# A hybrid decoder trunk on one core: the low halves of the last projection tile's weights move from VectorE to GpSimd

## The reference

```python
h = rms_norm(x, ln1_g[layer])
(a_q, a_ckv, a_kr, i_q, i_k, i_w, b_u, c_q, c_kv, c_gate) = jnp.split(h @ w_in[layer], offsets, axis=-1)
a_out = dsa_mixer(...)    # sparse attention with an indexer's top 64, rotary on parts
b_out = s5_mixer(b_u, ...)  # diagonal state-space model: scan over the positions
c_out = nsa_mixer(...)    # compressed, selected and window attention
x = x + concat(rms_norm(a_out), rms_norm(b_out), rms_norm(c_out)) @ w_out[layer]
x = x + square(relu(rms_norm(x, ln2_g[layer]) @ w_up[layer])) @ w_down[layer]
```

## Time and profile before

| | us |
|---|---|
| median of 3 runs (800.11 to 800.49) | 800.15 |
| the profiled execution | 800.82 |
| its span | 798.8 |
| busy: TensorE / VectorE / ScalarE / GpSimd | 687.8 / 524.1 / 362.2 / 316.4 |

### The profile page before, as it was taken

How to read it: one execution, slowest core, us unless ns; L and a number is a source line. 1 busy time by engine, 2 the same in 40 slices (tenths; PEclk the granted TensorE clock), 3 DMA queues, 4 the chain that set the end, 5 groups by cost and what they waited for, 6 DMA issues and landing times.

```text
span 798.8 us, 11006 instructions
## 1 busy us (share of the span) xinstructions
PE 687.8 (86%) x4020; PEld 606.3 (76%) x4020; DVE 524.1 (66%) x925; ACT 362.2 (45%) x656; POOL 316.4 (40%) x485
## 2 busy tenths in 40 slices
PE   2881944988989999999999697597998999999994
PEld 2771833976879999999978585476788999999983
DVE  5629999486385555666557999768447645555553
ACT  3550142366554454444436316155735544444441
POOL 5699993255305349999000444335510000000000
PEclk9995885799999999999999988689999999999998
DMA  9530310010168556556635350000125566666631
GB/s 258 172 105 0 111 52 1 1 53 27 54 185 246 196 186 185 167 184 201 210 108 169 105 163 1 1 27 27 54 89 166 167 203 191 187 185 188 186 127 80
DMA packets 51876, 100.25 MB, mean 126 GB/s; under 512 B 11093, under 2 KB 15902, under 8 KB 51822
## 3 DMA queue, kind: packets, MB, share of 16 engines
q1 hardware_dynamic: 48750, 96.40, 39.0%
q0 software_dynamic: 720, 1.97, 1.0%
q10 hardware_dynamic: 2352, 1.18, 0.6%
HBM read 98.48 MB, written 1.05 MB: 125 GB/s over the span
## 4 chain that ended last, share of the span: by engine, by line
PE 61%; DVE 25%; issue 6%; POOL 4%; ACT 2%; DMA 1%; DVEq 0%; SPq 0%; ACTq 0%; POOLq 0%
PE pb L1408 61%; DVE dtmp L978 6%; DVE w_lo L1051 4%; DVE scan L1119 2%; DVE dtmp L985 1%; DVE x L985 1%; DVE btab L1320 1%; POOL e L519 1%; DVE h_lo L985 1%; POOL bt L519 1%; DMA pos_i<-in_positions 1%; DVE top L1204 1%; DVE scan L978 1%; ACT btab L884 1%; DVE dtmp L1109 1%
## 5 line engine op out<-in xcount | busy, mean ns | idle before, releaser
L1051 DVE TENSOR_TENSOR w_lo<-raw,w_hi 128x1024 fp32r<-128x1024 f32 (+2 forms) x176 | 220.1, 1268 | 140.5 <-ACT w_hi L725 140.2
L725 ACT ACTIVATE w_hi<-raw 128x1024 fp32r<-128x1024 f32 (+2 forms) x184 | 188.2, 1028 | 255.0 <-PE pb L1408 255.0
L1408 PE MATMUL pb<-h_hi,w_hi 128*128 128x256 f32 x512 | 145.0, 283 | 1.8 <-DVE h_lo L985 1.8
L1408 PE MATMUL pb<-h_lo,w_hi 128*128 128x256 f32 x512 | 144.9, 283 | 0.0
L1408 PE MATMUL pb<-h_hi,w_lo 128*128 128x256 f32 x512 | 144.9, 283 | 0.0
L523 POOL TENSOR_SCALAR pst<-stat 128x2 f32<-128x2 f32 (+1 forms) x11 | 2.8, 255 | 307.5 <-ACT proj L729 278.7
L1408 PE MATMUL pb<-w_hi,h_hi 128*128 128x512 f32 (+2 forms) x224 | 86.0, 384 | 21.3 <-DVE w_lo L1051 20.4
L1408 PEld LDWEIGHTS pb<-h_hi,w_hi 128*128 128x128 f32 x512 | 98.2, 192 | 2.7 <-DVE w_lo L1051 2.2
L1408 PE MATMUL pb<-w_hi,z_hi 128*128 128x512 f32 x256 | 99.8, 390 | 0.0
L1408 PE MATMUL pb<-w_hi,z_lo 128*128 128x512 f32 x256 | 99.8, 390 | 0.0
L1408 PE MATMUL pb<-w_lo,z_hi 128*128 128x512 f32 x256 | 99.6, 389 | 0.0
(11 more groups left out here) (267 smaller groups left out, 1212.2 us busy)
## 6 DMA issues: line engine op xcount, KB each, us to landing
raw<-in_w_up SPq DMA_DIRECT2D x64, 512.0 KB, 3.8
raw<-in_w_down SPq DMA_DIRECT2D x64, 512.0 KB, 4.3
raw<-in_w_in SPq DMA_DIRECT2D x24, 512.0 KB, 4.6
raw<-in_w_out SPq DMA_DIRECT2D x16, 512.0 KB, 3.8
raw<-in_w_in SPq DMA_DIRECT2D x8, 308.0 KB, 3.1
raw<-in_w_in SPq DMA_DIRECT2D x8, 280.0 KB, 3.2
x<-in_x ACTq DMA_DIRECT2D x1, 1024.0 KB, 5.3
out<-x SPq DMA_DIRECT2D x2, 512.0 KB, 2.7
```

The source lines that it names most:

```text
L725: hi_made.by(act.activation(w_hi[:, n % RING, 0:width(n)], raw[:, n % RING, 0:width(n)], ACT.Copy))
L1051: lo_made.by(dve.tensor_tensor(w_lo[:, n % RING, 0:width(n)], raw[:, n % RING, 0:width(n)], w_hi[:, n % RING, 0:width(n)].bitcast(F32), AL ...
L1408: return pe.matmul(o, l, r, start=start, stop=stop, skip_group_check=True)
```

## The change

`lo_out` is defined ahead of the rotations, takes the width of the piece, and GpSimd calls it for pieces 16 to 19 between its rotations 1 and 2. VectorE's four calls between its rounds 1 and 2 go. This holds for both layers.

```diff
@@ GpSimd
                 rstd(L, 2, rkv[:], stat[:, 2:4], A_RANK)
+                def lo_out(n):
+
+                    pool.wait_ge(lo_made.sem, lo_made.at(L, n))
+                    pool.wait_ge(hi_made.sem, hi_made.at(L, n + 1))
+                    lo_made.by(pool.tensor_tensor(w_lo[:, n % RING, 0:width(n)], raw[:, n % RING, 0:width(n)],
+                                                  w_hi[:, n % RING, 0:width(n)].bitcast(F32), ALU.subtract))
+
+
                 for r in range(ROUNDS):
+                    if r == 2:
+                        for n in range(16, 20):
+                            lo_out(n)
                     pool.wait_ge(scanned.sem, scanned.at(L, r + 1))
...
-                def lo_out(n):
-
-                    pool.wait_ge(lo_made.sem, lo_made.at(L, n))
-                    pool.wait_ge(hi_made.sem, hi_made.at(L, n + 1))
-                    lo_made.by(pool.tensor_tensor(w_lo[:, n % RING, :], raw[:, n % RING, :],
-                                                  w_hi[:, n % RING, :].bitcast(F32), ALU.subtract))
...
@@ VectorE
                 for n in range(12, 16):
                     lo(n)
                 s5_round(1)
-                for n in range(16, 20):
-                    lo(n)
                 s5_round(2)
```

## The result

The changed kernel takes 810.34 us (median of four runs, 808.65 to 811.0) against 800.32 us: the ratio is 1.012, with a 95% interval from 1.0102 to 1.0138. It is slower by 10.0 us. The kernel before was run a fourth time beside it, so its median here is 800.32 and not 800.15. The profiled execution took 810.84 us.

What follows compares the result with a forecast made beforehand. The prediction took VectorE's queue to bound the kernel before the rotary block, with tile 4 becoming late; 5.4 us in layer 0 plus 3.0 in layer 1 made 8.4, so a median of 808.5 us, range 805.0 to 813.5.

Steps and rivals of the forecast that it cites:

- What bounds, and the slack: VectorE's queue sets the pace before the rotary block; tile 4's result has slack of 10.5 us in layer 0, 2.3 in layer 1.
- the two terms expected: Expected for "late" before its run: round 3 plus 2.6 us in layer 0, plus 1.3 to 1.7 in layer 1.
- GpSimd's price: One 560-column subtraction on GpSimd takes 1.45 us with VectorE idle, 1.7 beside its scans; bounds 1.3 and 2.0.
- Layer 0: Tile 4 waits for subtractions behind rotation 1; the rotary block ends near 126.2 instead of 120.76: +5.4 us, bounds +4 and +8.5.
- Layer 1: Subtractions run beside round 2's scans, tile 4 is late; the block ends at 494.9 instead of 491.89: +3.0 us, +2 to +4.9.
- The recovery in the block: In layer 0 rotation 2 slows only the rotary block's first 2.7 us; the rest runs undisturbed, against 7.9 us in all before.
- The first rival: GpSimd slows VectorE through the late block, 7.9 us wherever it starts: +8.5 and +4.9, 813.5 us; chance 0.13.
- hidden wait: Rival: block without GpSimd beside it and tile 4 at full clock, +0.7 and -2.1, about 799 us, no change; chance 0.04.
- relief: Rival: VectorE loses 3.7 us in layer 0, 0.4 in layer 1 if tile 4 is out in time: 796.1 us; chance 0.03.
- What was to cost nothing: Loads of pieces 20 to 23, `bu(3)`, the indexer's work, ScalarE's copies and the wider `lo_out` add no time.
- the margin of 3 us: In layer 0 the indexer's results come at about 129.7, before VectorE reads them after round 3 at some 132.5.
- a stretch between the layers that grows by more than 1 us: Sign of a wrong forecast: stretches behind 138.85 and its layer 1 counterpart grow or shrink by more than a microsecond.

Runs made afterwards that it cites:

- Layer 0 only: The change made in layer 0 alone, layer 1 as in the kernel before: 805.97 us, ratio 1.0079.
- layer 1 only: The change made in layer 1 alone, layer 0 as in the kernel before: 804.39 us, ratio 1.0053.
- late: The kernel before with one more wait: TensorE begins tile 4 only when GpSimd has ended rotation 1; 804.98 us, ratio 1.005.
- 8 columns: The changed kernel with each of GpSimd's four subtractions covering only 8 of 560 columns, the rest left out: 802.44 us, ratio 1.003.

## Why the prediction was right

It had 808.5 us, from 805.0 to 813.5, and slower at 0.93; measured were 810.34 and a second time 810.3. The chain from GpSimd's place in its queue over tile 4 and the block to round 3 is what the trace shows. The sum of the two layers, 8.4 us, was met at 8.3 in part because two errors cancel: layer 0 came out 0.5 lower and layer 1 0.4 higher.

*What bounds, and the slack.* VectorE's queue sets the pace, tile 4 has a slack of 10.5 and 2.3 us, and GpSimd's place behind rotation 1 overdraws it. "Layer 0 only", "layer 1 only" and "late" confirm it with costs in both layers, the 3.8 us of "late" against 3.9 to 4.3 by the two terms expected.

*GpSimd's price.* Taken: 1.45 us idle, 1.7 beside scans. Measured: 1.44 and 1.76. The estimate of 1.2 us from the Trainium skill (GPSIMD Engine Reference, Elementwise — side-by-side cycle accounting) was too low here, and the line between two rows of this kernel was the better guide.

*Layer 0.* Subtractions from 110.35 (forecast 110.2), tile 4 from 111.85 (111.7), copy from 120.14 (120.5), block from 121.05 (121.4), round 3 at 126.11 (126.2). These agree on the clock of the span, but rotation 0 began at 92.56 in this trace and not at 92.09; counted from it, each came about half a us sooner than forecast. The clock rose as after the 14.00 us wait: the window from 114 to 116 shows 0.52, the next full speed, so at about 115.9, 4.1 us after the start and not 5.2. Plus 5.4 was forecast; the traces have 4.9 and 5.1 by the measure from rotation 0, 5.35 by the clock of the span.

*Layer 1.* Whether the clock had fallen was called a toss and taken as fallen: the window from 484 to 486 has 0.64, so it fell at 484.6, 1.8 us ahead of tile 4. Forecast plus 3.0, measured plus 3.4, and 3.6 alone. The 0.4 is in rotation 2: it waits for the scans of round 2 and began 16.3 us after rotation 1, where 15.8 were assumed (469.20 to 485.0), so the block was slowed that much longer.

*The recovery in the block* was the step with most at stake, 3 us in layer 0. It came: 5.06 us, forecast 4.8. The first rival, a block of 7.9 us wherever it starts, is out for this kernel; with the subtractions one place earlier it was, at 10.7 us, worse than that rival.

*The rivals with hidden wait or relief.* The relief needed tile 4 out by 109.1, and the hidden wait a block without GpSimd beside it. VectorE stood before the block at 109.3 (forecast 109.1) and waited for 11.78 us, and rotation 2 ran into the block. That 109.3 was met is partly luck: round 2's sums took 0.9 us more than before (3.25 against 2.38), `cn` 1.0 less (1.30 against 2.32). It made no difference, as the wait behind it was longer.

*What was to cost nothing.* From round 3 to the first high half of piece 20 it is 28.45 us before and after in layer 0 (120.76 to 149.21, 126.11 to 154.56) and 28.4 in layer 1. So the loads, the indexer and `bu(3)` cost nothing, and the margin of 3 us held.

*What the sum missed.* The two layers make 8.3 to 8.5 us, as forecast; the medians differ by 10.0 and 9.9. Of the other 1.5 the profiles give no steady account. The span of the first pair differs by 10.3 us: 1.9 between the layers, where TensorE's clock was low near 215 and 242, 0.5 ahead of rotation 0, and 0.4 less behind layer 1's round 3. The 1.9 us, with the 0.4 of layer 1, are why round 3 of layer 1 came at 502.56 and not at 500.3. The second profile of the changed kernel is 9.0 us above the first of the kernel before, with 1.5 us ahead of rotation 0, and only 8.0 above the second. One of the prediction's own signs of being wrong, a stretch between the layers that grows by more than 1 us, thus came up in the first profile (1.9) and not in the second. It was set too tight, since the unaltered kernel moved by 1.0 there as well. As the surplus was in both comparisons of medians, it may still hang on the change in a way that these traces don't show. That stays open.

## What to carry to other kernels

Work moved to an engine with idle time pays by its place in that engine's queue: look at what stands ahead of it (here rotation 1, so that tile 4 came 16 us later) and what it pushes back (rotation 2), and hold both against the slack of whoever waits. Where two engines slow each other, a displaced operation costs or gives back whatever it now runs beside, and a wait can be refunded there: in layer 0 a block that began 8.2 us late ended 5.4 us late. With TensorE waiting for 16 us, layer 0 lost 1.2 us ("8 columns"), 2.7 ("late") or 4.9 (the change); what is behind the wait decides.

## What the runs showed of the hardware

- The slowing of VectorE by GpSimd goes by instructions here, not by columns. The block's twelve operations took 2.8 us alone ("8 columns"), 7.9 before, 10.7 and 11.1 beside GpSimd throughout. Where one is held up, an addition of 64 columns takes 1.24 us (0.23 alone) and one of 256 columns 1.37 (0.42 alone), about the length of one of GpSimd's 512-column operations (1.3). The Trainium skill (SBUF — State Buffer, Who interferes with whom) has it that a VectorE instruction with two inputs in SBUF contends with a GpSimd instruction that reads SBUF, that the ports they share are an exclusive lock, and that the order of issue decides who blocks. These durations agree with that. So does this: round 2's products, with one input in PSUM, took 1.87 us for three beside rotation 0 (99.12 to 100.99, before) and round 3's 1.88 with GpSimd idle.
- GpSimd is slowed far less: a rotation took 8.1 us alone and 9.8 beside VectorE's scans (10.2 in layer 1 beside low halves and round 2), while VectorE's four scans went from 2.44 us to 6.47.
- Four subtractions of 8 columns, with a semaphore's wait each, took 1.05 us on GpSimd with VectorE idle, 0.26 each, and four of 560 columns 5.74. So nearly all of the price is in the columns, 2.1 ns each.
- In the changed kernel's layer 1 TensorE stopped at 481.67 and its granted clock fell at 484.6, 2.9 us later; in the kernel before it stopped at 500.28 and the clock fell 4.8 us later. Ahead of tile 4 and of tile 3 it had fallen, and it rose 4.1 us (114 to 116: 0.52) and 5.2 us (84 to 86: 0.70) after the tile began.
- Runs of one kernel differ by 2.9 us (799.02 to 801.87, the kernel before) and up to 4.9 (800.79 to 805.72, "8 columns"), and the place of single low-clock stretches differs between profiles of the same kernel.
